# Attention in a one-core decoder trunk: raw probabilities are turned, and the value products are made by query rows

## The reference, cut to what matters

```python
sc = jnp.einsum('bqgrd,bgnd->bgrqn', qb, k_cmp)
p_c = masked_softmax(sc, cmp_end[None, :] <= tq[:, None])
o_c = jnp.einsum('bgrqn,bgnd->bqgrd', p_c, v_cmp)
...
o_s = jnp.einsum('bgrqkl,bgqkld->bqgrd', p_s, vs)      # selected blocks
...
o_w = jnp.einsum('bgrqk,bgkd->bqgrd', masked_softmax(sw, m_w), vw)
return gb[..., 0:1] * o_c + gb[..., 1:2] * o_s + gb[..., 2:3] * o_w
...
return o @ w_o
```

## Time and profile before

| | |
|---|---|
| median of 3 runs | 936.47 us (935.56 to 936.64) |
| the profiled execution | 937.43 us, with a span of 935.7 us |
| TensorE busy | 893.5 us, 95% of the span |
| VectorE, ScalarE busy | 584.6 us (62%), 513.2 us (55%) |
| granted TensorE clock | 0.999 of full speed |
| DMA | 138.29 MB, mean 148 GB/s |

### The profile page before, as it was taken

How to read it: one execution, slowest core, us unless ns; L and a number is a source line. 1 busy time by engine, 2 the same in 40 slices (tenths; PEclk the granted TensorE clock), 3 DMA queues, 4 the chain that set the end, 5 groups by cost and what they waited for, 6 DMA issues and landing times.

```text
span 935.7 us, 14029 instructions
## 1 busy us (share of the span) xinstructions
PE 893.5 (95%) x5289; PEld 757.9 (81%) x5289; DVE 584.6 (62%) x964; ACT 513.2 (55%) x911; POOL 55.5 (6%) x82
## 2 busy tenths in 40 slices
PE   6989999999999999999999899998889999999998
PEld 6989988788888878888888789886567888888876
DVE  6876985767676575555544676777757555554465
ACT  6645655666766474444533559356856544443452
POOL 6000230302000000000000000000000000000000
PEclk9999999999999999999999999999999999999999
DMA  9941211111124657677555555420034565654552
GB/s 341 339 141 40 91 46 46 46 46 47 46 86 143 209 169 226 227 231 231 197 173 176 187 180 174 136 91 1 1 116 155 185 189 186 190 193 158 195 186 93
DMA packets 105900, 138.29 MB, mean 148 GB/s; under 512 B 4586, under 2 KB 76787, under 8 KB 105843
## 3 DMA queue, kind: packets, MB, share of 16 engines
q1 hardware_dynamic: 103650, 130.15, 42.8%
q0 software_dynamic: 2160, 7.36, 2.0%
q10 hardware_dynamic: 32, 0.01, 0.0%
HBM read 136.45 MB, written 1.05 MB: 147 GB/s over the span
## 4 chain that ended last, share of the span: by engine, by line
PE 77%; DVE 9%; ACT 9%; issue 2%; DMA 1%; SPq 0%; ACTq 0%; DVEq 0%
PE ps L528 16%; PE ps L530 16%; PE ps L529 16%; PE ps L507 5%; DVE w_lo L1607 4%; PE ps L512 4%; PE ps L514 4%; PE ps L513 4%; ACT w_hi L1138 3%; PE ps L739 2%; PE ps L759 2%; PE ps L1024 1%; DVE gdn L1674 1%; ACT qkvT L1541 1%; DMA w_raw<-in_ple_w_in 1%
## 5 line engine op out<-in xcount | busy, mean ns | idle before, releaser
L1607 DVE TENSOR_TENSOR w_lo<-w_raw,w_hi 128x2048 fp32r<-128x2048 f32 (+2 forms) x100 | 220.7, 2207 | 197.3 <-ACT w_hi L1138 197.3
L1138 ACT ACTIVATE w_hi<-w_raw 128x2048 fp32r<-128x2048 f32 (+2 forms) x100 | 184.5, 1845 | 184.0 <-PE ps L530 143.3
L528 PE MATMUL ps<-w_hi,x_hi 128*128 128x512 f32 x480 | 193.1, 402 | 5.6 <-DVE x_lo L1638 2.1
L530 PE MATMUL ps<-w_hi,x_lo 128*128 128x512 f32 x480 | 187.6, 391 | 0.0
L529 PE MATMUL ps<-w_lo,x_hi 128*128 128x512 f32 x480 | 187.1, 390 | 0.0
L528 PEld LDWEIGHTS ps<-w_hi,x_hi 128*128 128x128 f32 x480 | 90.2, 188 | 26.4 <-issue 4.8
L530 PEld LDWEIGHTS ps<-w_hi,x_lo 128*128 128x128 f32 x480 | 90.1, 188 | 19.5
L529 PEld LDWEIGHTS ps<-w_lo,x_hi 128*128 128x128 f32 x480 | 90.4, 188 | 16.7
L512 PE MATMUL ps<-x_hi,w_hi 128*128 128x256 f32 x320 | 91.4, 286 | 1.4 <-DVE w_lo L1607 1.0
L513 PE MATMUL ps<-x_lo,w_hi 128*128 128x256 f32 x320 | 90.5, 283 | 0.0
L514 PE MATMUL ps<-x_hi,w_lo 128*128 128x256 f32 x320 | 90.5, 283 | 0.0
(11 more groups left out here) (312 smaller groups left out, 1468.9 us busy)
## 6 DMA issues: line engine op xcount, KB each, us to landing
w_raw<-in_ffn_w_in SPq DMA_DIRECT2D x88, 512.0 KB, 4.5
w_raw<-in_ffn_w_out SPq DMA_DIRECT2D x40, 512.0 KB, 4.4
w_raw<-in_gdn_w_in SPq DMA_DIRECT2D x28, 512.0 KB, 4.6
gdn<-in_gdn_w_in SPq DMA_DIRECT2D x20, 512.0 KB, 7.6
w_raw<-in_gdn_w_out SPq DMA_DIRECT2D x16, 512.0 KB, 4.2
w_raw<-in_ple_w_gate SPq DMA_DIRECT2D x16, 512.0 KB, 4.6
w_raw<-in_kv_w SPq DMA_DIRECT2D x12, 512.0 KB, 4.0
qkvT<-in_cmp_w POOLq DMA_DIRECT2D x8, 512.0 KB, 5.0
```

Source lines behind the costliest of these rows:

```text
L528: mm(o, hi, w_h, start=first and kk == 0, stop=False, skip_group_check=True)
L530: return mm(o, lo, w_h, start=False, stop=end and kk == n - 1, skip_group_check=True)
L1138: A(whi[:, place(stage, q), c0:c0 + n], ring_raw(u) if stage == "qkv" else raw[:, q, 0:n], ACT.Copy).then_inc(S["hi_done"], 1)
L1607: V.tensor_tensor(wlo[:, s, c0:c0 + n], ring_raw(u) if stage == "qkv" else raw[:, q, 0:n], whi[:, s, c0:c0 + n], ALU.subtract).then_inc(S[ ...
```

## The change

Probabilities are turned as the exponentials leave them. VectorE copies bank 7 (`turned` on VectorE) and ScalarE only bank 6. A new `token_output(p)` makes the value products with the turned probabilities (128x128) as the stationary operand and the values (64 columns) moving: 12 products into bank 0, laid out as [query tile and branch, head, feature], with query rows on the partitions. `head_weights(p)` makes the factors, eight for each query row of a pair, and `weighted(p)` multiplies the whole bank by them in one VectorE instruction into osc. The new `output(p)` then turns these rows and adds the branches: for each query tile two products with osc as the stationary operand and the identity moving, and the compressed branch on top as before. It always uses bank 1.

The order changes with it. On TensorE the loop is token_output(p-1), scores(p+1, 0), turned(p, 0), output(p-1), scores(p+1, 1), turned(p, 1) for p > 2; pairs 0 and 1 are output in p = 2. token_output(7) stands inside the output projection, ahead of its k = 2. In the DeltaNet's `conv` one semaphore is dropped and its increments go to another one.

```diff
             def turned(p, e):
 
+                pe.wait_ge(S["p_act"], 2 * p + e + 1)
                 for b in range(2):
-                    pe.wait_ge(S["pw_dve"], 4 * p + 2 * e + b + 1)
                     if p or e:
-                        pe.wait_ge(S["pts_act"], 4 * p + 2 * e + b - 1)
+                        pe.wait_ge(S["pts_dve" if b else "pts_act"], 2 * p + e)
...
-            def output(p):
+            def token_output(p):
 
                 g, par = p // 2, p % 2
-                pe.wait_ge(S["pts_act"], 4 * p + 4)
+                pe.wait_ge(S["pts_act"], 2 * p + 2)
+                pe.wait_ge(S["pts_dve"], 2 * p + 2)
                 if p == 0:
                     pe.wait_ge(S["pct_sb"], 1)
-                    pe.wait_ge(S["fx_dve"], NG)
-                if p == 1:
-                    pe.wait_ge(S["cs_dve"], 10)
-                if p >= 2:
-                    pe.wait_ge(S["alo"], p - 1)
-                o = [ps[halves[e], par, 0:T] for e in range(2)]
+                else:
+                    pe.wait_ge(S["osc_dve"], p)
+                o = bank(0, TT * 2, 2, ND)
                 for b in range(2):
                     vb = [vtk[:, s, b, ND * g:ND * g + ND] for s in range(2)]
                     for e in range(2):
-                        mm(o[e], vb[0], pts[:, par, e, b, 0:2, :].rearrange("p s q -> p (s q)"), start=b == 0, stop=False,
+                        mm(o[:, b, e, :], pts[:, par, e, b, 0, :], vb[0], start=b == 0 and e == 0, stop=False,
                            skip_group_check=True)
-                    for e in range(2):
-                        mm(o[e][:, P:T], vb[1], pts[:, par, e, b, 2, :], start=False, stop=False, skip_group_check=True)
+                        mm(o[:, 2 + b, e, :], pts[:, par, e, b, 1, :], vb[0], start=False, stop=False, skip_group_check=True)
+                        last = mm(o[:, 2 + b, e, :], pts[:, par, e, b, 2, :], vb[1], start=False, stop=b == 1 and e == 1,
+                                  skip_group_check=True)
+                last.then_inc(S["avt_ps"], 1)
+
+            def output(p):
+
+                g, par = p // 2, p % 2
+                pe.wait_ge(S["osc_dve"], p + 1)
...
+                    pe.wait_ge(S["alo"], p)
+                for a in range(TT):
+                    for b in range(2):
+                        mm(bank(1, TT, P)[:, a, :], osc[:, par, 2 * a + b].rearrange("p e d -> p (e d)"), ident[:, :],
+                           start=a == 0 and b == 0, stop=False, skip_group_check=True)
...
+            def head_rows(k):
+                if k == 2:
+                    token_output(7)
+                pe.wait_ge(S["alo"], k + 1)
...
# ScalarE, turned(p, e)
-                for b in range(2):
-                    act.wait_ge(S["ptr_ps"], 4 * p + 2 * e + b + 1)
-                    A(pts[:, p % 2, e, b], bank(6 + b, 3, P), ACT.Copy).then_inc(S["pts_act"], 1)
+                act.wait_ge(S["ptr_ps"], 4 * p + 2 * e + 1)
+                A(pts[:, p % 2, e, 0], bank(6, 3, P), ACT.Copy).then_inc(S["pts_act"], 1)
...
# VectorE
-                for b in range(2):
-                    V.tensor_scalar(pr0[:, par, e, b, :], pr0[:, par, e, b, :], l[:, b:b + 1], None, ALU.mult)
-                    V.tensor_scalar(pr1[:, par, e, b, :], pr1[:, par, e, b, :], l[:, 2 + b:3 + b], None,
-                                    ALU.mult).then_inc(S["pw_dve"], 1)
+            def turned(p, e):
+
+                if p >= 2:
+                    dve.wait_ge(S["avt_ps"], p - 1)
+                dve.wait_ge(S["ptr_ps"], 4 * p + 2 * e + 2)
+                V.tensor_copy(pts[:, p % 2, e, 1], bank(7, 3, P)).then_inc(S["pts_dve"], 1)
+
+            def weighted(p):
+
+                i = 2 * (p % 2)
+                dve.wait_ge(S["rl_dve"], 3 * p + 3)
+                dve.wait_ge(S["avt_ps"], p + 1)
+                V.tensor_tensor(osc[:, p % 2], bank(0, TT * 2, 2, ND),
+                                over(hst[:, i:i + 2, 0, :].rearrange("p e c -> p c e"), 3, ND), ALU.mult).then_inc(S["osc_dve"], 1)
...
             for p in range(1, 8):
-                weights(p, 0)
+                if p > 1:
+                    weighted(p - 1)
                 if p < 7:
                     maxima(p + 1, 0, 0)
                     maxima(p + 1, 1, 0)
-                weights(p, 1)
+                turned(p, 0)
+                if p == 2:
+                    out_lo(0)
                 if p < 7:
                     maxima(p + 1, 0, 1)
                     maxima(p + 1, 1, 1)
+                turned(p, 1)
+                head_weights(p)
```

More of the change, by code:

```diff
@@ L250, in build @@
                      "gt_ps gt_dve gt_done cs_ps cs_dve cs_act pct_ps pct_sb fx_dve "
-                     "sc_ps mx_dve p_act rl_dve pw_dve ptr_ps av_ps ahi alo out_st").split():
+                     "sc_ps mx_dve p_act rl_dve pts_dve ptr_ps avt_ps osc_dve av_ps ahi alo out_st").split():
             S[name] = sem(name)
@@ L1063, in output @@
                     for e in range(2):
-                        mm(o[e], vb[0], pts[:, par, e, b, 0:2, :].rearrange("p s q -> p (s q)"), start=b == 0, stop=False,
+                        mm(o[:, b, e, :], pts[:, par, e, b, 0, :], vb[0], start=b == 0 and e == 0, stop=False,
                            skip_group_check=True)
-                    for e in range(2):
-                        mm(o[e][:, P:T], vb[1], pts[:, par, e, b, 2, :], start=False, stop=False, skip_group_check=True)
+                        mm(o[:, 2 + b, e, :], pts[:, par, e, b, 1, :], vb[0], start=False, stop=False, skip_group_check=True)
[5 more added lines that the diff above has]
+                pe.wait_ge(S["osc_dve"], p + 1)
+                if p == 0:
+                    pe.wait_ge(S["cs_dve"], 10)
+                    pe.wait_ge(S["fx_dve"], NG)
+                else:
+                    pe.wait_ge(S["alo"], p)
[3 more added lines that the diff above has]
+                           start=a == 0 and b == 0, stop=False, skip_group_check=True)
                 for e in range(2):
-                    last = mm(o[e], vz[:, g, 2 * par + e, :], pct[:, g, :], start=False, stop=True, skip_group_check=True)
+                    last = mm(ps[halves[e], 1, 0:T], vz[:, g, 2 * par + e, :], pct[:, g, :], start=False, stop=True,
+                              skip_group_check=True)
                 last.then_inc(S["av_ps"], 1)
@@ L1089, in _ @@
                 if p > 1:
-                    output(p - 1)
+                    token_output(p - 1)
                 if p < 7:
@@ L1094, in _ @@
                     scores(p + 1, 0)
+                if p == 2:
+                    output(0)
                 turned(p, 0)
+                if p > 2:
+                    output(p - 1)
                 if p < 7:
@@ L1576, in _ @@
             for p in range(1, 8):
-                if p > 1:
-                    out_hi(p - 1)
+                if p == 2:
+                    out_hi(0)
                 turned(p, 0)
@@ L1582, in _ @@
                 turned(p, 1)
-                if p == 1:
-                    out_hi(0)
+                if p > 2:
+                    out_hi(p - 1)
                 if p == 3:
@@ L1588, in _ @@
                     exps(p + 1)
+                if p == 2:
+                    out_hi(1)
                 if p == 1:
@@ L1665, in conv @@
             def conv(u):
-                s, n0 = u % 4, 4 * u
+                s = u % 4
                 dve.wait_ge(S["tap_done"], 2 * u + 2)
@@ L1675, in conv @@
                             in1=late, op0=ALU.mult, op1=ALU.add).then_inc(
-                                S["conv_done"] if (j, n) == (0, 1) else S["conv_extra"] if j == 0 else S["conv_dve"], 1)
+                                S["conv_done"] if (j, n) == (0, 1) else S["conv_dve"], 1)
             def logit_copy(n, b, count):
@@ L2152, in _, with head_weights @@
             n_rl = [0]
[L2154 to L2159, removed]
-                V.reciprocal(l, l).then_inc(S["rl_dve"], 1)
[L2161 to L2165, removed]
-                for b in range(2):
-                    V.tensor_scalar(pr0[:, par, e, b, :], pr0[:, par, e, b, :], l[:, b:b + 1], None, ALU.mult)
-                    V.tensor_scalar(pr1[:, par, e, b, :], pr1[:, par, e, b, :], l[:, 2 + b:3 + b], None,
-                                    ALU.mult).then_inc(S["pw_dve"], 1)
+            def head_weights(p):
+                i = 2 * (p % 2)
+                dve.wait_ge(S["p_act"], 2 * p + 2)
+                l = hst[:, i:i + 2, 2, :]
+                V.reciprocal(l, l).then_inc(S["rl_dve"], 1)
+                dve.wait_ge(S["rl_dve"], 3 * p + 1)
+                for e in range(2):
+                    head = 2 * p + e
+                    w2, l2 = (hst[:, i + e, v, :].rearrange("p (a b) -> p a b", a=TT) for v in (0, 2))
+                    stt(out=w2, in0=l2, scalar=1e30, in1=gates[:, :, 3 * head + 1:3 * head + 3], op0=ALU.min,
+                        op1=ALU.mult).then_inc(S["rl_dve"], 1)
@@ L2171, in out_lo @@
             def out_lo(p):
```

(14 more changed lines are left out.)

19 lines of the change are left out of this document (12 added, 7 removed).

## The result

The changed kernel takes 960.06 us (median of 4 runs, 955.55 to 961.37) against 936.56 us before: ratio 1.0243, 95% interval 1.023 to 1.0256. It is slower, as forecast, but 23.5 us and not 14.4, and outside the range of 944.5 to 956.5.

What follows compares the result with a forecast made beforehand. TensorE was taken to bound the kernel, 56.29 of 65.58 us busy in the attention stage. Steady passages of 8.90 us against 6.83, with start and projection, gave +14.4 on 936.47: 950.9 us, range 944.5 to 956.5.

Steps and rivals of the forecast that it cites:

- the schedule: Attention stage followed pair by pair on TensorE: the projection's second half starts at 706.5 us, was 692.08, so +14.4 us.
- output: Per pair on TensorE: four identity products 0.88 us, compressed-branch products 0.43, about 0.04 for the array change; 1.35 us together.
- the turn ahead of it: Turn of one head on TensorE, ahead of the output products: 0.80 us, taken to stay as before.
- late scores to next token products: From late scores' start until TensorE can start token products: 1.38 + 1.21 + 0.55 + 0.05 = 3.19 us.
- passage: One steady round of TensorE's attention loop: 2.69 + 0.87 + 0.80 + 1.35 + 3.19 = 8.90 us, against 6.83.
- Token products set by their weights: TensorE, 24 records a pair: 128-column weights, not the 64 moving columns, set 0.112 us each, 2.69 us together.
- the cheap rival: Token products cost 0.055 us a record, 1.31 us a pair; an 8.1 us loop binds; +6, 942.5 us; chance 0.09.
- The wait for VectorE's copy behind the maxima: TensorE waits 1.1 us a passage, replacing 0.70, because VectorE copies the second turn after the late scores' maxima.
- The waits of pairs 0 and 1: Loop's start: pair 1's token products wait about 0.85 us for bank 0; query unit starts +0.45 us later.
- The second loop of 8.1 us: Exponentials 2.43, early scores 0.87, turn 0.80, output 1.35, 2.65 until ScalarE is free; binds if token products are cheap.
- TensorE's idle time in the stage: TensorE's idle time in the attention stage, 9.3 us before, falls to some 6 to 7 us.
- The dear rival: Full-width products on TensorE cost a turn's 0.134 us a record: +0.7 a pair, +5.6 in all, 956.5 us; chance 0.12.

Runs made afterwards that it cites:

- The changed kernel's second profile: The changed kernel run once more, unaltered, for comparison on one chip: 960.23 us (956.64 to 961.35), its profiled execution at 956.64 us.

## Why the prediction was wrong

The direction and the schedule were right; the size was off by 9 us. The step that failed is a silent one. I had read a granted clock of 1.00 in the kernel before and let every duration of the sum stand at that level. In the changed kernel it does not stay there, and that costs 5.8 us. A smaller miss, 1.75 us, lies in the terms of the sum.

The account, from the start of the first compressed scores (L1001; L1002 after) to the second half of the projection's first weights: before 692.08 - 622.74 = 69.34 us, after 714.99 - 623.70 = 91.29, so +21.95. The rest of the 22.6 us between the two profiled executions lies outside the stage (0.97 us of later start ahead of it, 0.2 us less behind it). That later start is scatter: the stage starts anywhere between 621.34 and 623.79 us in the thirteen profiled executions, and at 621.64 in the kernel with the conv semaphore alone.

- **The clock, not forecast: 5.8 us.** The same code with 128 columns shows what the two stretches cost. From the token products of pair 1 to the late scores of pair 3 it is 656.93 - 646.08 = 10.85 us after, and 652.40 - 646.22 = 6.18 with 128 columns; 4.7 us. From the token products of pair 6 to the last turn it is 6.53 and 5.44; 1.1 us. The changed kernel's second profile agrees: its clock was down for about half as long, and its stage took 711.36 - 623.20 = 88.16 us, between the 91.29 here and the 709.50 - 623.79 = 85.71 with 128 columns.
- **The schedule: 16.15 us, forecast 14.4.** The terms in a passage: token products 2.80 (2.69 forecast; the records are 0.112 apart, and 0.11 goes with the change to the half array of the scores), output 1.57 (1.35 forecast), the turn ahead of it 0.72 (0.80), late scores to next token products 3.23 (3.19), passage 9.18 (8.90). The largest miss is the output. Its identity products cost about what I had priced, 0.112 a record for 0.110; what I had left out, but for 0.04, is the changes of how the array is split. The records of one group end with such a change where the next group works on a halved array, and a start-to-start price holds it. The last four of the eight identity records show it, on TensorE's timeline from 675.5 on:

```profile
675.26 0.61 PE L1081 MATMUL ps<-ident,scr 128*128 128x128 f32 x4
675.80 0.44 PE L1084 MATMUL ps<-qkvT 128*64 128x256 f32 x2
```

Four records at 0.112 would end at 675.71; the compressed products start 0.09 later. They themselves take 676.39 - 675.80 = 0.59 us, where they took 0.43 between neighbours of their own split. Together that is the 0.22 over forecast. Over eight pairs token products and output are 2.6 us more than forecast, and the cheaper turns give 0.6 back; small differences at pairs 0 to 3 make the rest.
- **Token products set by their weights: right.** 30, 64 and 128 moving columns have the same 0.112 us. The Trainium skill's rule that I had set beside it ("TensorE: Matmul & The Clock Gate", section "LDWEIGHTS (loading the stationary operand)") held within 5%; the cheap rival is dead.
- **The wait for VectorE's copy behind the maxima: right,** 1.08 us for 1.1, and shown by moving the copy.
- **The waits of pairs 0 and 1:** 0.97 us for 0.85 at bank 0; from the start of the stage, the query unit started 0.27 us later than before (630.51 - 623.70 against 629.28 - 622.74), for 0.45.
- **The second loop of 8.1 us: right,** 8.19 with half of the token products. TensorE's idle time in the stage is as forecast too: 87.54 - 80.59 = 6.95 us from the first turn (627.45) to 714.99.
- **The dear rival** (956.5) is dead, and its price was a misreading. It took 0.134 a record from a turn, 0.80/6; but the records of a turn are 0.109 apart in the trace, and the rest is the changes of the split in front of and behind it. Where full-width products follow, the turn costs 0.72.
- **A label:** by the order in the code the passage of the earlier trace rows is p = 5, and the prediction's "pair 6" is pair 5. No sum depends on it.

Without a fall of the clock the forecast would have been low by 3 us and inside its range (954.14 with 128 columns). With it, nothing in the range's working could hold the result: none of my cases had the clock in it, although the change puts 24 records of 64 columns where 16 of 128 and 256 columns had stood, and a wait of 1.08 us a passage ahead of them where 0.70 had been.

What exactly makes the clock fall is only bounded by these runs. Each of the eight falls that the profiles show in the stage (five profiles of four kernels, all with 64 columns there) begins at the token products: one as the wait ahead of them ends, the others 1.9 to 2.7 us behind the end of a wait of 1.08 us. With 128 columns the clock held in the stage in all four profiled kernels, with the same waits in three of them; with 64 columns and waits of at most 0.77 us it held in one. Idle time in sum does not explain it: the kernel before idles more in this stage, 9.3 us against 6.95, has waits of 1.06 and 1.08 us in it too (up to 646.45 and 661.39 on TensorE's timeline), and no fall. And the fall outside the stage, at 531 us behind a wait of 1.90 us, came with products of 512 columns. So narrow products are not needed, and not enough by themselves; how waits and columns weigh against each other was not told apart. The place and the number of falls differ between executions of one kernel.

## What to carry to other kernels

An f32 product with 128 columns of weights cost the same 0.112 us a record here with 30, 64 and 128 moving columns, so put the wide operand on the moving side. Turning a product round to save work on other engines was paid for on TensorE nearly in full here, and TensorE was the engine near its bound. Give each change between full and halved array a term of its own, about 0.1 us in these rows, and don't read it into the price of a record. When a change makes TensorE's work narrower or puts waits between it, give the granted clock a case of its own in the forecast, and price it from rows at both levels. The profitable edit was the small one: fill a wait of the engine in the chain (0.70 us on ScalarE) with work that it would otherwise do later in the same chain.

## What the runs showed of the hardware

- More columns in the same products made a kernel faster: 954.14 us with 128 moving columns, 960.06 with 64; the lower clock costs the latter 5.8 us. Four added products of 512 columns in a wait took 5 us off (954.83).
- Once the clock had fallen, at the end of the 0.97 us wait, TensorE was busy throughout the stretch at 0.50 (9.92 of 9.92 us), and the clock stayed down for 10 us all the same, while the engine worked through narrow token products, scores and identity products.
- A clock fall needs no narrow product: with 128 columns in the token products it fell at 531 us, behind a wait of 1.90 us and among products of 512 columns.
- A change from the full array to halved columns added 0.09 us between two products (675.80 - 675.71, identity to compressed products), and one to halved rows as much (682.42 - 682.10 is 0.32 us for two records of 0.112 and the change).
- A wait on two semaphores was put down to ScalarE, whose copy was the earlier of the two; moving the copy on VectorE shortened it from 1.08 to 0.77 us.
